# One turn per head: the head stage of a hybrid attention encoder, from a loop with woven steps to unrolled turns with spread steps

## The reference, cut to what matters

```python
def _gated_delta(q, k, v, g, beta, s0, chunk):         # group B, for each head
    gc = jnp.cumsum(g, axis=-1)
    decay = jnp.exp(jnp.where(causal, gc[..., :, None] - gc[..., None, :], -jnp.inf))
    kb = k * beta[..., None]
    a_mat = jnp.where(strict, jnp.einsum('bnhid,bnhjd->bnhij', kb, k) * decay, 0.0)
    rhs = jnp.concatenate([v * beta[..., None], kb * jnp.exp(gc)[..., None]], axis=-1)
    sol = lax.linalg.triangular_solve(a_mat + eye, rhs, left_side=True, lower=True, unit_diagonal=True)
    u, w = sol[..., :DV], sol[..., DV:]
    ...
    def step(s, inp):                                  # one chunk after the other
        v_new = u_n - w_n @ s
        o = qg_n @ s + qk_n @ v_new
        s = s * jnp.exp(gl_n) + kd_n.T @ v_new
        return s, o
...
    conv_out = silu(causal depthwise conv of width 4 over q, k, v of group B)
    q_b = _l2norm(q_b) * DK_B ** -0.5;  k_b = _l2norm(k_b)
    o_b = _rmsnorm(o_b, gnorm_w) * silu(z_b)
    # group A: softmax(q k^T - slope |t - s|) v over the selected keys, times silu(z_a)
```

## Time and profile before

| | us |
|---|---|
| median of 3 runs | 3342.03 (3327.34, 3342.03, 3343.69) |
| the profiled execution, span | 3344.3 |
| PE busy in it | 2967.6 (89%) |
| DVE busy | 1357.6 (41%) |
| ACT busy | 1025.5 (31%) |
| POOL busy | 887.9 (27%) |

### The profile page before, as it was taken

The page is one execution under the profiler, slowest core; times in us unless marked ns, Lnnn a source line. Parts: engine busy times, 40 slices in busy tenths (PEclk is TensorE's granted clock), DMA queues, the critical chain, the costliest instruction groups (busy, mean ns, idle before and its releaser), DMA issues. The chain is left out here.

```text
span 3344.3 us, 46103 instructions
## 1 busy us (share of the span) xinstructions
PE 2967.6 (89%) x16691; PEld 2657.3 (79%) x16691; DVE 1357.6 (41%) x2550; ACT 1025.5 (31%) x1995; POOL 887.9 (27%) x607
## 2 busy tenths in 40 slices
PE   4999899999999999999995588788878885799997
PEld 3999598998989899899995477667767774487876
DVE  6000101917463260705000667767776763214042
ACT  4111112213121211212112455565555553222221
POOL 6222021121212122121222223313422330155553
PEclk6999699999999999999997699999999997599998
DMA  3221222121212212122224111121121013346553
GB/s 129 62 65 60 43 69 73 49 72 49 67 57 64 62 60 73 56 66 63 69 64 133 36 49 50 41 69 34 35 69 48 27 41 88 125 155 208 175 180 120
DMA packets 271700, 255.47 MB, mean 76 GB/s; under 512 B 58712, under 2 KB 222752, under 8 KB 269152
## 3 DMA queue, kind: packets, MB, share of 16 engines
q1 hardware_dynamic: 261536, 208.80, 21.1%
q10 hardware_dynamic: 10048, 45.27, 3.3%
HBM read 190.48 MB, written 63.56 MB: 76 GB/s over the span
## 5 line engine op out<-in xcount | busy, mean ns | idle before, releaser
L394 PE MATMUL bank<-hH,wL 128*128 128x384 f32 (+1 forms) x2928 | 981.5, 335 | 14.9 <-POOL wL L311 14.9
L395 PE MATMUL bank<-hL,wH 128*128 128x384 f32 (+1 forms) x2928 | 980.1, 335 | 0.0
L396 PE MATMUL bank<-hH,wH 128*128 128x384 f32 (+1 forms) x2928 | 979.9, 335 | 0.0
L311 POOL TENSOR_TENSOR wL<-raw,wH 128x512 fp32r<-128x512 f32 x244 | 314.6, 1290 | 1388.7 <-ACT wH L328 1388.7
L394 PEld LDWEIGHTS bank<-hH,wL 128*128 128x128 f32 (+1 forms) x2928 | 550.1, 188 | 19.2 <-issue 18.5
L395 PEld LDWEIGHTS bank<-hL,wH 128*128 128x128 f32 (+1 forms) x2928 | 550.0, 188 | 0.8
L396 PEld LDWEIGHTS bank<-hH,wH 128*128 128x128 f32 (+1 forms) x2928 | 550.0, 188 | 0.7
L328 ACT ACTIVATE wH<-raw 128x512 fp32r<-128x512 f32 x244 | 154.2, 632 | 1019.3 <-PE bank L396 964.4
L1949 POOL TENSOR_TENSOR owL<-oraw,owH 128x2048 fp32r<-128x2048 f32 x48 | 225.5, 4700 | 271.4 <-ACT owH L1969 271.4
L506 DVE TENSOR_SCALAR score<-relued,w_idx 128x512 f32<-128x512 f32 (+3 forms) x10 | 7.8, 778 | 683.5 <-ACT relued L353 683.1
L1026 POOL TENSOR_TENSOR Bm<-A,keep_level 128x512 f32<-128x512 f32 x168 | 207.8, 1264 | 216.6 <-DVE A L1547 121.3
(11 more groups left out here) (297 smaller groups left out, 4028.8 us busy)
## 6 DMA issues: line engine op xcount, KB each, us to landing
raw<-in_w_in SPq DMA_DIRECT2D x240, 256.0 KB, 2.8
oraw<-in_w_out SPq DMA_DIRECT2D x48, 1024.0 KB, 5.0
proj_scratch<-ptbuf ACTq DMA_DIRECT2D x60, 576.0 KB, 2.8
xin<-proj_scratch SPq DMA_DIRECT2D x24, 512.0 KB, 4.8
mraw<-mix_scratch SPq DMA_DIRECT2D x12, 768.0 KB, 5.6
x<-in_x_prompt SPq DMA_DIRECT2D x8, 1024.0 KB, 5.0
out_y_prompt<-yv ACTq DMA_DIRECT2D x8, 1024.0 KB, 4.0
ox<-in_x_prompt SPq DMA_DIRECT2D x8, 768.0 KB, 6.6
```

The source lines that it names most:

```text
L311: pool.tensor_tensor(wL[c % 2][:, :, :], raw[c][:, :, :], wH[c % 2][:, :, :].bitcast(F32), ALU.subtract).then_inc(low_ready, 1)
L394: pe.matmul(o, low, hH[:, kk, tok], start=first, stop=False)
L395: pe.matmul(o, high, hL[:, kk, tok], start=False, stop=False)
L396: last = pe.matmul(o, high, hH[:, kk, tok], start=False, stop=end)
```

## The change

The loops and the separate code for first and last head go: eight heads are unrolled, and a function `iteration(i)` places steps of three heads in one turn by fractions of the turn, sorted: states, sample and output of head i; the whole delta preparation and the whole attention of head i+1; convolution, natural turns and unit vectors of head i+2. The turns run from -2 to 7. The steps themselves change too:

- Convolution: prompt and samples lie in one row (`xc`, 1179 columns with pads), one DVE instruction for each tap. The convolution's weights and the decays of the chunk ends (`egl`) are made for all heads in `prepare_heads`.
- Decay: PE adds the mask and the two sums in PSUM (one bf16 product, two fp32r products of 256 columns for each tile); ACT takes the exponents straight from there, with the gate as bias; DVE multiplies gram and decay for two tiles in one instruction. `D_gates` is gone, gates are read from the kept table.
- Attention: bias and maximum are one DVE instruction for up to 512 columns (`tensor_tensor_reduce`), the probabilities are normalised on DVE before they are transposed (`A_norm`), values come out transposed, so that `A_turn_o` and `A_scale` go.
- States: banks 0 and 1 alone; the output's addition stands in the same step as its product. All solves come ahead of the states.
- Levels: three banks for both halves, one step between the halves in place of two. Natural turns: two banks (0 and 1, which states, sample and output use too). The output's squares are one ACT instruction and a DVE reduction.

The diff, cut to its core:

```diff
+def spread(first, last, steps):
+    return [(first + (last - first) * (i + 0.5) / len(steps), step) for i, step in enumerate(steps)]
+
+def iteration(i):
+    placed = []
+    if 0 <= i < H:
+        h = i
+        states = []
+        for t in range(NT):
+            states += [("M_read", h, t), ("M_state", h, t)]
+        sample = [(s, h, 0) for s in ("S_state", "S_turn", "S_new", "S_out")]
+        out = [("O_square", h, 0), ("O_norm", h, 0)] + [("O_out", h, g) for g in range(3)]
+        placed += spread(0.0, 0.52, states) + spread(0.52, 0.64, sample) + spread(0.64, 0.74, out)
+        placed += [(0.53, ("L_store_state", h, 0)), (0.65, ("L_store_sample", h, 0)), (0.75, ("L_store_mixb", h, 0))]
+    if 0 <= i + 1 < H:
+        h = i + 1
...
+        placed += spread(0.0, 0.07, turns) + spread(0.07, 0.26, grams) + spread(0.26, 0.30, first)
+        placed += spread(0.30, 0.93, levels) + spread(0.93, 1.0, solves)
+        attend = []
+        for t in range(-1, NT):
...
+            attend += logits[:1] + turn[:1] + biases[:1] + logits[1:] + turn[1:] + biases[1:]
+            if t + 1 < NT:
+                attend += [("A_exp", h, t + 1)]
+            if t >= 0:
+                attend += [("A_values", h, t)]
+            if t + 1 < NT:
+                attend += [("A_norm", h, t + 1)]
+            if t >= 0:
+                attend += [("A_gate", h, t)]
+        placed += spread(0.0, 0.95, attend)
+        placed += [(0.01, ("L_state", h, 0)) if h == 0 else (0.79, ("L_state", h, 0))]
+        placed += [(0.02, ("L_zb", h, 0)) if h == 0 else (0.84, ("L_zb", h, 0)), (0.97, ("L_store_mixa", h, 0))]
+    if 0 <= i + 2 < H:
+        h = i + 2
+        taps = [("N_pads", h, 0)] + [("N_tap", h, n) for n in range(3)]
...
+        placed += spread(0.05, 0.12, taps) + spread(0.12, 0.46, conv) + spread(0.46, 0.50, gates)
+        placed += spread(0.74, 0.90, natural) + spread(0.90, 1.0, norms)
+        placed += [(0.30, ("L_za", h, 0)) if h > 1 else (0.0, ("L_za", h, 0)), (0.78, ("L_store_tails", h, 0))]
+        placed += [(0.0, ("L_qa", h, 0)) if h == 0 else (0.92, ("L_qa", h, 0))]
+    if 0 <= i < H:
+        placed += [(0.50, ("O_silu", i, 0))]
+    if 0 <= i + 3 < H:
+        placed += [(0.80, ("L_x", i + 3, 0))]
+    return [step for _, step in sorted(placed, key=lambda item: item[0])]
...
 # PE
-                    if t >= 2:
+                    if t:
                         wait(pe, o_ready, h, t)
-                    pe.matmul(big[:, 2 + t % 2, 0:P], qkT[:, t, 0, :], S[:, :], start=True, stop=True)
+                    pe.matmul(big[:, 1, 0:P], qkT[:, q_slot(h), t, :], S[:, :], start=True, stop=True)
...
+                            pe.matmul(out, K["identb"][:, :], K["maskTN"][:, s, halves, :], start=True, stop=False)
+                            for part in range(2):
+                                last = pe.matmul(out, K["glog"][:, h, part, t:t + 1].to_broadcast([P, P]), K["cum2"][:, s, :, :], start=False, stop=part == 1)
...
 # ACT
-                    do(de[t % 2][:, :, :], dd[t % 2][:, :, :], ACT.Exp).then_inc(decay_ready.sem, 1)
+                    for t in range(lo, hi):
+                        do(de[p % 2][:, t - lo, t_half, :], cum[:, t - lo, t_half, :], ACT.Exp, bias=K["gates"][:, h, G_NEG, t:t + 1])
+                        last = do(de[p % 2][:, t - lo, n_half, :], cum[:, t - lo, n_half, :], ACT.Exp, bias=K["gates"][:, h, G_POS, t:t + 1], scale=-1.0)
...
 # DVE
-                    V.scalar_tensor_tensor(out=y[:, n, 0:SEQ], in0=xin[:, n, j:j + SEQ], scalar=w, in1=y[:, n, 0:SEQ], op0=ALU.mult, op1=ALU.add).then_inc(convolved.sem, 1)
-                    ys = y[:, n, SEQ:].rearrange("p (b t) -> p b t", b=DEC_B)
-                    V.scalar_tensor_tensor(out=ys, in0=xsm[:, n, :, j:j + DEC_T], scalar=w, in1=ys, op0=ALU.mult, op1=ALU.add).then_inc(convolved.sem, 1)
+                    V.scalar_tensor_tensor(out=y[:, n, :], in0=xc[:, n, j:j + YC], scalar=K["cw"][:, n * H + h, 3 * DEC_B + j:3 * DEC_B + j + 1], in1=y[:, n, :], op0=ALU.mult, op1=ALU.add).then_inc(convolved.sem, 1)
...
                 def state(h, t):
                     wait(dve, ds_done, h, t + 1)
...
-                    if t:
-                        add_out(h, t - 1)
-                    if t == NT - 1:
-                        add_out(h, t)
+                    wait(dve, o1_ready, h, t + 1)
+                    V.tensor_tensor(o[:, t, :], o[:, t, :], big[:, 1, P:2 * P], ALU.add).then_inc(o_ready.sem, 1)
...
-                    V.tensor_tensor(lg[t % 2][:, 0:w], src, K["alibi"][:, SEQ - w:SEQ], ALU.add).then_inc(lg_ready.sem, 1)
...
-                    V.tensor_reduce(am[:, t, 0:1], lg[t % 2][:, 0:w], AX_X, ALU.max).then_inc(max_ready.sem, 1)
...
+                    V.tensor_tensor_reduce(out=lg[t % 2][:, c:e], in0=big[:, LG_BANK + i % 2, 0:e - c], in1=K["alibi"][:, at + c:at + e], scale=-SCALE, scalar=smallest,
+                                           op0=ALU.add, op1=ALU.min, accum_out=am[:, t, q // 4:q // 4 + 1]).then_inc(lg_ready.sem, 1)
...
+                def normalise(h, t):
+                    w = (t + 1) * P
+                    wait(dve, exp_ready, h, t + 1)
+                    V.reciprocal(am[:, t, 3:4], am[:, t, 2:3]).then_inc(inv_ready.sem, 1)
+                    wait(dve, inv_ready, h, t + 1)
+                    V.tensor_scalar(lg[t % 2][:, 0:w], lg[t % 2][:, 0:w], am[:, t, 3:4], None, ALU.mult).then_inc(p_scaled.sem, 1)
...
 # GpSimd
-                over_heads(pool, {"D_keys": scale_keys, "D_first": first, "D_level": levels, "D_sample_out": sample_mask})
+                run({"D_keys": scale_keys, "D_first": first, "D_level": levels, "S_new": sample_mask})
```

More of the change, by code:

```diff
@@ L640, in _ @@
                 last.then_inc(turned, 1)
+                pe.wait_ge(rows_loaded, 32)
+                for half in range(2):
+                    for j in range(3 * H // 2):
+                        last = pe.transpose(cwp[half][:, j * ROWS:(j + 1) * ROWS], conv_rows[:, half * 3 * H // 2 + j, :], ident[0:ROWS, 0:ROWS])
+                    last.then_inc(rows_turned, 1)
                 pe.wait_ge(kv_loaded, 16)
@@ L793, in run_heads, with whole_order @@
+def whole_order():
+    order = [("L_x", 0, 0)]
+    for i in range(-2, H):
+        order += iteration(i)
+    return order
 def run_heads(nc, io, scratch, keep, ident):
@@ L889, in wait_before, with run @@
-        def wait_before(eng, sig, h, k):
-            eng.wait_ge(sig.sem, sig.before(h, k))
-        def part(t, q):
-            return PARTS.index((t, q)) + 1
+            if sig.upto(h, k) > 0 and h >= 0:
+                eng.wait_ge(sig.sem, sig.upto(h, k))
         def quad(b):
             return big[:, b, :].rearrange("p (t c) -> p t c", t=4)
-        def run(order, steps, h):
-            for name, k in order:
+        def run(steps):
+            for name, h, k in order:
                 if name in steps:
-                    steps[name](h + {"N": 1, "P": -1}.get(name[0], 0), k)
@@ L1191, in _ @@
[L1191 to L1196 removed]
+                    wait(act, lg_ready, h, PARTS_TO[t])
@@ L1267, in values_of @@
-                def values_of(kv):
-                    def values(h, t):
-                        wait(pe, p_ready, h, part(t, t // 4 * 4))
-                        if t:
-                            wait(pe, mixa_ready, h, t)
-                        for kb in range(t + 1):
-                            last = pe.matmul(big[:, 7, 0:P], PT[t % 2][:, kb, :], K["vN"][:, kb, kv, :], start=(kb == 0), stop=(kb == t))
-                        last.then_inc(pv_done.sem, 1)
-                    return values
@@ L1426, in out @@
                     last.then_inc(o_turned.sem, 1)
-                def steps(kv):
-                    return {
-                        "N_rows": rows, "N_tails": tails, "N_turn": natural, "A_logits": logits_of(kv), "A_turn_p": turn_p, "A_turn_p2": lambda h, t: turn_p(h, t, 4),
-                        "A_values": values_of(kv), "A_turn_o": turn_o, "D_turn": qk_turn, "D_decay": decay, "D_first": first,
-                        "D_level": level, "D_solve": solve, "D_sample_state": sample_state, "D_sample_turn": sample_turn,
-                        "D_sample_out": sample_out, "D_read": read, "D_state": state, "P_out": out, "D_solve_sample": solve_sample, "N_done": prepared}
@@ new lines, in turn_p @@
+                def turn_p(h, i):
+                    t, q = PARTS[i]
+                    wait(pe, p_scaled, h, t + 1)
+                    if q:
+                        wait(pe, p_ready, h, i)
+                    elif t:
+                        wait(pe, mixa_ready, h, t)
+                    else:
+                        wait(pe, mixa_ready, h - 1, NT)
+                    for kb in range(q, min(q + 4, t + 1)):
+                        last = pe.transpose(quad(PV_BANK)[:, kb - q, :], lg[t % 2][:, kb * P:(kb + 1) * P], ident[:, :])
+                    last.then_inc(p_turned.sem, 1)
@@ new lines, in values @@
+                def values(h, t):
```

(11 more changed lines are left out.)

995 lines of the change are left out of this document (448 added, 547 removed).

## The result

The changed kernel takes 3312.86 us (median of 5 runs, 3311.04 to 3318.51); the kernel before, run beside it, 3343.69. The ratio is 0.9909, with a 95% interval of 0.9886 to 0.9932: about 31 us faster, where 89 were forecast. The profiled execution spans 3311.7 us (before: 3344.3).

A forecast was written before the change was run, and what follows sets the result against it. No single engine bounds a head: the bound moves, with about 16 of 119 us in waits. Turns of 104 us and the end turns sum to 849 us against 932; with the lead-in minus 89, so 3253 us, range 3191 to 3333.

The forecast's parts named there:

- The slower rival: Rival, chance 0.10: DVE's waits for ACT's copy at the state's output addition hold up PE; 118 us a turn, 3363 us.
- term (b): State's output addition: DVE waits for ACT's copy, eight waits of 0.5 to 1 us, 4 to 8 us a turn.
- the turn: One turn with steps of three heads: 104 us, bounds 94 and 114; each us moves the result by 7.8.
- The factor 1.15: In-order waits: a head takes 119 / 103.3 = 1.15 times its busiest engines; applied to 91.4 it gives 105 us.
- a table of issue times: Turn's steps laid out by fractions, busiest engine of each tenth taken: sum 91.4 us, waits to come on top.
- (a): Border of turns: the next turn's first transposes wait for head i+2's unit vectors; 2 to 5 us lost.
- the clock: PE's granted clock in a turn: 3 us added because it isn't always full.
- the third tenth: Third tenth of a turn: DVE busiest at 11.5 us with convolution, gram products and states.
- DVE's work: DVE's work in a turn: falls from 84.3 to 67.6 us.
- the normalisation: DVE's eight new instructions normalising the probabilities: plus 1 us, bounded above by 6.0; waits for POOL estimated beside the sum.
- the fused logits: Logits' add and maximum on DVE become 12 fused instructions: 6.9 us, minus 5.1.
- still in step: Rival, chance 0.12: few banks make every step wait for the one before; 112 us a turn, 3318 us.

The follow-up runs named there:

- late_add: Changed kernel with DVE's output addition moved into the next state's read, and PE's queries-times-state product into the state's step; 3311.7 us, ratio 0.9872.
- late_conv: The edits of late_add and conv_late together on the changed kernel; 3268.7 us, ratio 0.9762.
- conv_late: Changed kernel with the convolution at 0.35-0.72 instead of 0.12-0.46, taps later too, SiLU, natural turns and unit vectors shifted; 3258.6 us, ratio 0.9729.
- no_conv: Changed kernel, own order, with the convolution left out but for one column of each DVE instruction (outputs not the layer's); 3251.8 us, ratio 0.9703.
- no_scale: Changed kernel with the normalisation of the probabilities left out but for one column (outputs not the layer's); 3295.0 us, ratio 0.9832.
- border: Changed kernel with natural turns and unit vectors placed earlier and the next head's state zeroed at the output step's end; 3327.0 us, ratio 0.9954.
- tuned: The spaced kernel with the attention shifted to 0.03-1.0 and the next head's state zeroed earlier; 3309.2 us, ratio 0.9895.
- out_later: The conv_late kernel with the output norm at 0.64-0.68 and its three transpositions at 0.71-0.75; 3257.4 us, ratio 0.9716.
- spaced: The conv_late kernel with more room between sample, output norm and its transpositions, natural turns and unit vectors slightly later; 3274.6 us, ratio 0.9802.
- taps_early: The conv_late kernel with ACT's taps kept at 0.05-0.12, where the changed kernel has them; 3291.0 us, ratio 0.9840.

## Why the prediction was right and wrong

**What held.** Faster, and inside the range, but by a third of the forecast, and by another way. The change "doesn't make PE's work smaller; it can only fill its holes", says the prediction; PE's holes went from 22.4 to 21.5 us in turn 3, and its busy time from 96.6 to 91.4. So the direction came right in part by luck. The lead-in ends 7.4 us earlier (8 were summed, 2 given back). Turns 6 and 7 take 127.3 us (97 + 36). PE's price for the decay sums is as taken: three products of a tile are 0.35 us apart (2322.50, 2322.85, 2323.21), so 3.2 us a turn. Loads are hidden: none of PE's waits in turn 3 ends with one. The slower rival fell: DVE stood 8.6 us at eight additions, 1.08 us each, above the 0.75 put in and far below the 2.2 that decided (115.4 us a turn would have been the limit: that rival takes 8 us for the lead-in where the sum has 6). Taking these waits away was worth 1.1 us a turn in late_add and nothing in late_conv, so the 4 to 8 us of term (b) were charged to the wrong wait. Behind the heads 3.2 us went that no step had (537.0 to 533.8 us).

**What failed: the turn**, 104 in the sum and 113.9 measured; six turns are 683 us in place of 624, and turn -1 99.2 in place of 92. These 66 us are the whole miss, less what the ends gave. Two steps are behind it.

*The factor 1.15 was put on the wrong base.* It came from busy times, in which PE had 96.6 us with its tails and at its granted clock; I put it on a table of issue times at full clock, with 83 us for PE. Turn 3's busiest engines, tenth by tenth, are busy 8.9, 9.5, 11.3, 10.9, 9.8, 10.2, 9.2, 11.2, 10.5 and 7.5 us, in all 99.0, and 112.9 / 99.0 is 1.14; the head before, cut in tenths too, gives 119.0 / 104.7 = 1.14. So the factor held, and the table's sum of 91.4 didn't. PE's busy time (by chance 91.4 us as well) was 8.4 above its issue time of 83. The terms added one by one fell short as well: 3.5 for (a), 6 for (b) and 3 for the clock are 12.5 us above the table's sum, and a turn measured 22.5 above it. The page before showed both kinds of time, and only like goes with like.

*A tenth was priced as its busiest engine, as if the others ran beside it.* At 11.5 us the third tenth came out right (11.3), and that hid what mattered: PE got 4.31 us of work done in it and had to do the rest later, where it was full anyway (11.25 of 11.30 in the eighth tenth). PE waits for DVE's small instructions of the states and of the first level; the convolution it doesn't wait for, and that stood ahead of them in DVE's queue. conv_late and no_conv show its size: 7.8 and 7.6 us a turn, most of the 9.9 that were missing. The two steps are two views of one loss and don't add up: in conv_late the tenths' busiest engines sum up to 93.2 us, and 105.4 / 93.2 is still 1.13.

DVE's work was 72.1 us and not 67.6. Of the 4.5, 2.7 are the normalisation: 6.5 us, less the 2.8 of the old scaling, where plus 1 was taken; its upper bound, 6.0, was passed; 1.0 are the fused logits (4.7 + 2.2 + 1.0 = 7.9, where 6.9 were taken). no_scale shows that 4.8 us of the normalisation counted for 1.2 us a turn.

The *still in step* rival named this time (112 us a turn, 3318), but not this cause: it had PE wait everywhere for small copies. PE's waits became fewer and longer (29 in the head before, two of them over 2 us; 11 in turn 3, five of them over 2 us), and DVE ends most of those in turn 3. What was to show the forecast wrong did show: PE busy 81% of a turn, where over 85% was put. Its sign of the border, a long wait for unit vectors, is there too (2.50 us); no edit here that shortened it (border, tuned) made a turn shorter.

## What to carry to other kernels

When several heads share a turn, look in each stretch at what stands in the *queue* of the engine that the others wait for: work that nobody needs soon (here a convolution for the next but one head) belongs where that engine has room, and its place, with that of its taps, was worth 7.8 us a turn, as much as leaving it out. A wait taken away need not be worth its length: what was done here against single waits (late_add, border, out_later, spaced) gained 1.1 us a turn at best and cost up to 3.1, as other waits grew. So move one step at a time, and compare PE's busy and idle time of a turn, not the list of waits; the busy time moves with the granted clock, so look at several turns. And never multiply a factor got from busy times with a sum of issue times.

## What the runs showed of the hardware

**Behind the same wait PE works at either clock level.** The four passes of the sample's update (L1338, two products) took 1.98 us behind a wait of 1.04 us in the changed kernel. In conv_late they stand behind a wait of 2.57 or 2.58 us in every turn: in turn 1 they took 1.95 us, in a tenth with a granted clock of 1.00, and in the other five 3.40 to 3.62, in turn 3 in a tenth with 0.84, so with part of it at the 1.2 GHz level:

```profile
2127.60 1.95 PE L1338 MATMUL big<-vmask,kd 128*128 128x512 f32 x4 [2.58 <-DVE uw L1481]
...
2338.39 3.62 PE L1338 MATMUL big<-vmask,kd 128*128 128x512 f32 x4 [2.58 <-DVE uw L1481]
```

```profile
2333.20:2343.70 10.50, 7.92 (x38) 5.19 (x38) 7.74 (x17) 0.99 (x4) 3.25 (x3) 0.84 0.00 0
```

So the length of a wait alone doesn't tell what the work behind it takes, and PE's busy time for the same order ranges from 90.4 to 96.4 us a turn in taps_early alone. Before, with 22.4 us of idle time and 29 waits, the clock of a head was 0.96.

**DVE's one-operand scaling stands behind GpSimd (POOL).** In the changed kernel the normalisation of 128 columns took longer than that of 1024; POOL's instruction at its side ended at 2314.77, DVE's at 2314.85:

```profile
2313.90 0.95 DVE L1531 TENSOR_SCALAR lg<-lg,am 128x128 f32<-128x128 f32 x1
...
2406.37 0.76 DVE L1531 TENSOR_SCALAR lg<-lg,am 128x1024 f32<-128x1024 f32 x1
```

```profile
2312.66 2.11 POOL L996 TENSOR_TENSOR vb<-nat,keep_gates 128x1152 f32<-128x1152 f32 x1
```

This is what the Trainium skill says (SBUF — State Buffer, section "Who interferes with whom"): a `tensor_scalar` in the 2-port mode takes the pair of ports that DVE and GpSimd share. The trace agrees: 128, 384 and 512 columns beside POOL took 0.95, 1.24 and 1.30 us; 256, 640 and 1024 without it 0.35, 0.55 and 0.76. By a line through those without it, the three are some 2.3 us too long together, an estimate; the prediction's, beside its sum, was 1.7 us a turn. With that in the sum the normalisation would have been 2.8 + 1 + 1.7 = 5.5 us, against the 6.5 measured.
